# Pairs of tiles in the norms between blocks, and weight splits ahead of them, in a two-network fp32 kernel

## The reference

```python
for i in range(DEPTH):                      # DEPTH = 2
    mod = (c_act @ ada_w[i] + ada_b[i])[:, None, :]
    sh_m, sc_m, gt_m, sh_f, sc_f, gt_f = jnp.split(mod, 6, axis=-1)
    ...
    h = rmsnorm_2(x, norm_g[i, 0]) * (1.0 + sc_m) + sh_m
    y = rglru_mixer(h, ...) if i % 2 == 0 else gla_mixer(h, ...)
    x = x + gt_m * rmsnorm_2(y, norm_g[i, 1])
    h = rmsnorm_2(x, norm_g[i, 2]) * (1.0 + sc_f) + sh_f
    y = conv_ffn(h, ffn_w_up[i], ffn_conv_w[i], ffn_conv_b[i], ffn_w_down[i])
    x = x + gt_f * rmsnorm_2(y, norm_g[i, 3])
```

## Time and profile before

| | |
|---|---|
| median of 3 runs | 1875.89 us (1875.47 to 1876.12) |
| the profiled execution | 1869.09 us, its span 1867.3 us |
| PE busy | 1794.7 us (96%) |
| DVE busy | 1445.4 us (77%) |
| ACT busy | 885.7 us (47%) |
| granted TensorE clock, mean | 0.995 |

### The profile page before, as it was taken

How to read it: one execution, slowest core, us unless ns; L and a number is a source line. 1 busy time by engine, 2 the same in 40 slices (tenths; PEclk the granted TensorE clock), 3 DMA queues, 4 the chain that set the end, 5 groups by cost and what they waited for, 6 DMA issues and landing times.

```text
span 1867.3 us, 29958 instructions
## 1 busy us (share of the span) xinstructions
PE 1794.7 (96%) x11480; PEld 1583.2 (85%) x11480; DVE 1445.4 (77%) x2557; ACT 885.7 (47%) x1528; POOL 0.2 (0%) x4
## 2 busy tenths in 40 slices
PE   4999999999999999999999999998998999999997
PEld 2788887767888887988888999987998979989997
DVE  5649985558899988797867898777988888779864
ACT  3322334456222333443456555575665356556552
POOL 0000000000000000000000000000000000000000
PEclk8999999999999999999999999999999999999999
DMA  9422322113677776353222996443656924235652
GB/s 345 136 91 90 93 66 68 49 54 130 204 263 257 246 252 224 126 158 113 91 69 74 325 312 216 136 148 114 201 184 229 357 69 158 91 104 192 196 170 85
DMA packets 242909, 302.78 MB, mean 162 GB/s; under 512 B 6080, under 2 KB 224448, under 8 KB 242256
## 3 DMA queue, kind: packets, MB, share of 16 engines
q1 hardware_dynamic: 242768, 300.87, 48.8%
HBM read 299.79 MB, written 1.05 MB: 161 GB/s over the span
## 4 chain that ended last, share of the span: by engine, by line
PE 37%; DVE 12%; ACT 5%; issue 3%; DMA 1%; DVEq 0%; ACTq 0%
PE bank L567 8%; PE bank L562 8%; PE bank L564 8%; DVE w_lo L1744 3%; PE bank L538 3%; PE bank L540 3%; PE bank L539 3%; ACT w_hi L1129 2%; DVE work L2347 1%; DVE work L2353 1%; ACT work L1115 1%; DVE stats L1678 1%; PE bank L513 1%; DVE arena L2306 1%; PE bank L928 0%
## 5 line engine op out<-in xcount | busy, mean ns | idle before, releaser
L1744 DVE TENSOR_TENSOR w_lo<-ring,w_hi 128x1024 fp32r<-128x1024 f32 (+2 forms) x444 | 499.3, 1132 | 192.8 <-ACT w_hi L1129 189.5
L1129 ACT ACTIVATE w_hi<-ring 128x1024 fp32r<-128x1024 f32 (+2 forms) x444 | 433.9, 985 | 167.0 <-PE bank L567 102.7
L562 PE MATMUL bank<-h_hi,w_hi 128*128 128x256 f32 (+2 forms) x2374 | 419.2, 318 | 2.0 <-ACT w_hi L1129 1.6
L567 PE MATMUL bank<-h_hi,w_lo 128*128 128x256 f32 (+2 forms) x2374 | 411.4, 315 | 2.5 <-DVE w_lo L1744 2.5
L564 PE MATMUL bank<-h_lo,w_hi 128*128 128x256 f32 (+2 forms) x2374 | 411.4, 315 | 0.0
L562 PEld LDWEIGHTS bank<-h_hi,w_hi 128*128 128x128 f32 x2374 | 345.8, 188 | 36.1 <-ACT w_hi L1129 3.9
L567 PEld LDWEIGHTS bank<-h_hi,w_lo 128*128 128x128 f32 x2374 | 347.0, 188 | 32.4 <-DVE w_lo L1744 2.7
L564 PEld LDWEIGHTS bank<-h_lo,w_hi 128*128 128x128 f32 x2374 | 347.0, 188 | 29.9
L1115 ACT ACTIVATE work<-bank 128x512 f32<-128x512 f32 (+1 forms) x142 | 70.1, 507 | 280.8 <-PE bank L567 214.5
L1115 ACT ACTIVATE arena<-bank 128x256 f32<-128x256 f32 (+4 forms) x121 | 55.2, 457 | 221.1 <-PE bank L567 147.8
L538 PE MATMUL bank<-h_hi,w_hi 128*128 128x256 f32 (+2 forms) x426 | 127.0, 298 | 20.9 <-DVE h_lo L1697 9.1
(11 more groups left out here) (260 smaller groups left out, 2111.2 us busy)
## 6 DMA issues: line engine op xcount, KB each, us to landing
ring<-in_w_in SPq DMA_DIRECT2D x86, 1024.0 KB, 5.4
arena<-in_ada_w_t SPq DMA_DIRECT2D x96, 512.0 KB, 6.1
ring<-in_ffn_w_up SPq DMA_DIRECT2D x44, 1024.0 KB, 5.1
ring<-in_w_branch SPq DMA_DIRECT2D x32, 512.0 KB, 4.7
arena<-in_w_mod_t SPq DMA_DIRECT2D x32, 512.0 KB, 5.3
ring<-in_ffn_w_down SPq DMA_DIRECT2D x16, 1024.0 KB, 5.1
ring<-in_gla_w_in SPq DMA_DIRECT2D x12, 1024.0 KB, 5.4
ring<-in_w_out SPq DMA_DIRECT2D x8, 1024.0 KB, 5.4
```

Source lines behind the costliest of these rows:

```text
L562: pe.matmul(out[:, 0:n], w[0][:, k, :], hi(k, n), start=k == 0, stop=False)
L567: m = pe.matmul(out[:, 0:n], w[1][:, k, :], hi(k, n), start=False, stop=k == tiles - 1)
L1129: nc.scalar.activation(w_hi[u % PARTS][:, 0:src.shape[1], :], src, ACT.Copy)\
L1744: step(nc.vector.tensor_tensor(w_lo[u % PARTS][:, 0:nk, :], src, w_hi[u % PARTS][:, 0:nk, :].bitcast(F32), ALU.subtract), f"lo {u}", *(["u ...
```

## The change

1. `post` and `normed2` work on pairs of tiles. `post` becomes 8 tensor_tensor operations on 512 columns, with the reciprocal broadcast over the pair. The gain of y leaves `post`; ScalarE applies it in `store_y`, which now squares first and then stores with an Identity. In `normed2` the pairs are only multiplied by the reciprocal; ScalarE applies gain and shift in place, tile by tile, and makes `h_hi` of a pair with one copy. In the two ffn hand-overs (`single`) the first two tiles keep the old form.
2. ScalarE squares x in pairs; TensorE sums them in `sum_pairs`. Second fillers go from 11 (12 in hand-over 2) to 7 products.
3. The 16-wide z is made from the shifted tiles in full float32, 8 products in place of 16 on the parts.
4. VectorE makes the low parts of the next block's first three units (two in hand-over 2) ahead of `post`, the rest behind `normed2`. In hand-over 2 ScalarE makes the high parts of those two units ahead of the stores of the last two output tiles.

```diff
@@ -316,6 +316,12 @@
+        def two(t):
+            return t[:].rearrange("p (a s) -> p a s", a=2)
+        def pair_tile(k):
+            return dve_t[k // 2][:, S * (k % 2):S * (k % 2) + S]
@@ -613,6 +619,15 @@
+            def sum_pairs(name):
+                out = open_bank(name)
+                for k in range(KT):
+                    pe.wait_ge(*scalar.did(f"sq {name}.{k // 2}"))
+                    m = pe.matmul(out[:, 0:S], ones_pp, act_t[k // 2][:, S * (k % 2):S * (k % 2) + S],
+                                  start=k == 0, stop=k == KT - 1)
+                m.then_inc(*tensor.does("filled " + name))
@@ -866,8 +881,8 @@
                 keep_clock(9)
-                sum_all(f"n3 {l}", S, KT)
-                keep_clock(11)
+                sum_pairs(f"n3 {l}")
+                keep_clock(7)
@@ -942,14 +957,13 @@
             keep_clock(9)
-            sum_all("n2 1", S, KT)
-            keep_clock(12)
+            sum_pairs("n2 1")
+            keep_clock(7)
...
             for k in range(KT):
-                both_parts("n2 1")(k)
-                pe.matmul(out[0:16, 0:S], wz[:, k, :], h_hi[:, k, 0:S].bitcast(F32), start=k == 0, stop=False)
-                m = pe.matmul(out[0:16, 0:S], wz[:, k, :], h_lo[:, k, 0:S].bitcast(F32), start=False, stop=k == KT - 1)
+                pe.wait_ge(*scalar.did(f"shifted n2 1.{k}"))
+                m = pe.matmul(out[0:16, 0:S], wz[:, k, :], pair_tile(k), start=k == 0, stop=k == KT - 1)
@@ -959,7 +973,7 @@
                 for n in range(GLA_H):
-                    project(f"gla{nm} {n}", S)
+                    project(f"gla{nm} {n}", S, ready=both_parts("n2 1") if nm == "q" and n == 0 else None)
@@ -1489,25 +1503,42 @@
-            def pre_norm(name, ready, l, q, first):
+            def pre_norm(name, ready, l, q, first, single):
...
                 warm_sqrt(name)
-                square_all(name, S, KT, lambda k: xT[:, k, 0:S], ready)
+                for i in range(KT // 2):
+                    act.wait_ge(*ready(2 * i + 1))
+                    nc.scalar.activation(two(act_t[i]), xT[:, 2 * i:2 * i + 2, 0:S], ACT.Square)\
+                        .then_inc(*scalar.does(f"sq {name}.{i}"))
                 deviation(name, S, D)
-                modulated(name, (0,), lambda k, g: mod2[l][:, 12 * q + k:12 * q + k + 1])
-            def store_y(tag, k):
+                gain, shift = gain2[l][:, q, :], mod2[l][:, 12 * q:12 * q + KT]
+                for k in range(2 if single else 0):
+                    act.wait_ge(*vector.did(f"normed {name}.{k}"))
+                    nc.scalar.activation(h_hi[:, k, 0:S], pair_tile(k), ACT.Identity, bias=shift[:, k:k + 1])\
+                        .then_inc(*scalar.does(f"hi {name}.{k}"))
+                for k in range(2 if single else 0, KT, 2):
+                    act.wait_ge(*vector.did(f"normed {name}.{k}"))
+                    for i in (k, k + 1):
+                        a = nc.scalar.activation(pair_tile(i), pair_tile(i), ACT.Identity, scale=gain[:, i:i + 1],
+                                                 bias=shift[:, i:i + 1])
+                    a.then_inc(*scalar.does(f"shifted {name}.{k}", f"shifted {name}.{k + 1}"))
+                    act.wait_ge(*scalar.did(f"shifted {name}.{k}"))
+                    nc.scalar.activation(h_hi[:, k:k + 2, 0:S], two(dve_t[k // 2]), ACT.Copy)\
+                        .then_inc(*scalar.does(f"hi {name}.{k}", f"hi {name}.{k + 1}"))
+            def store_y(tag, k, l, q):
...
                 act.wait_ge(*tensor.did("filled " + name))
-                nc.scalar.activation(yT[:, k, :], bank(name)[:, 0:S], ACT.Copy)
-                nc.scalar.activation(sq8[:, k, :], bank(name)[:, 0:S], ACT.Square)\
-                    .then_inc(*scalar.does(name, "emptied " + name))
-            def block_out(tag, src, ready):
+                nc.scalar.activation(sq8[:, k, :], bank(name)[:, 0:S], ACT.Square).then_inc(*scalar.does(name))
+                nc.scalar.activation(yT[:, k, :], bank(name)[:, 0:S], ACT.Identity, scale=gain2[l][:, q, k:k + 1])\
+                    .then_inc(*scalar.does("emptied " + name))
+            def block_out(tag, src, ready, l):
...
                     first_units(f"y {tag}.0")
+                act.wait_ge(*vector.did(f"gain2 {l}"))
...
@@ -1556,8 +1587,10 @@
                         split_to(unit_of[f"down {l}.{c + 1}.0.1"])
+                    elif l == 0:
+                        split_to(unit_of["glaq 1"])
                     for j in range(2):
-                        store_y(f"ffn {l}", 2 * c + j)
+                        store_y(f"ffn {l}", 2 * c + j, l, 3)
...
@@ -1719,15 +1752,48 @@
-            def normed2(name, l, q):
+            def by_two(row):
+                return row.unsqueeze(1).broadcast_to([P, 2, S])
+            def normed2(name, l, q, single):
                 inverse(name, S)
-                tile, low = normed(name, (0,), lambda k, g: gain2[l][:, q, k:k + 1],
-                                   lambda k, g: mod2[l][:, 12 * q + k:12 * q + k + 1])
-                for k in range(KT + 2):
-                    if k < KT:
-                        tile(k)
-                    if k >= 2:
-                        low(k - 2)
+                def pair(k):
+                    step(nc.vector.tensor_tensor(two(dve_t[k // 2]), xT[:, k:k + 2, 0:S], by_two(stat2[:, 0:S]), ALU.mult),
+                         f"normed {name}.{k}")
+                def pair_low(k):
+                    dve.wait_ge(*scalar.did(f"hi {name}.{k}"))
+                    step(nc.vector.tensor_tensor(h_lo[:, k:k + 2, 0:S], two(dve_t[k // 2]),
+                                                 h_hi[:, k:k + 2, 0:S].bitcast(F32), ALU.subtract),
+                         f"lo {name}.{k}", f"lo {name}.{k + 1}")
+                def one(k):
+                    step(nc.vector.scalar_tensor_tensor(pair_tile(k), xT[:, k, 0:S], gain2[l][:, q, k:k + 1],
+                                                        stat2[:, 0:S], ALU.mult, ALU.mult), f"normed {name}.{k}")
+                def one_low(k):
+                    dve.wait_ge(*scalar.did(f"hi {name}.{k}"))
+                    step(nc.vector.scalar_tensor_tensor(h_lo[:, k, 0:S], pair_tile(k), mod2[l][:, 12 * q + k:12 * q + k + 1],
+                                                        h_hi[:, k, 0:S].bitcast(F32), ALU.add, ALU.subtract),
+                         f"lo {name}.{k}")
+                if single:
+                    one(0)
+                    one(1)
+                    pair(2)
+                    one_low(0)
+                    one_low(1)
+                    pair(4)
+                    pair_low(2)
+                    pair(6)
+                    pair_low(4)
+                    pair_low(6)
+                else:
+                    for k in range(0, KT, 2):
+                        pair(k)
+                    for k in range(0, KT, 2):
+                        pair_low(k)
@@ -2298,17 +2364,18 @@
-            def post(tag, l, q):
+            def post(tag):
                 inverse(f"ys {tag}", S)
-                for n in range(KT + 1):
+                for n in range(0, KT + 2, 2):
                     if n < KT:
-                        step(nc.vector.scalar_tensor_tensor(yT[:, n, :], yT[:, n, :], gain2[l][:, q, n:n + 1],
-                                                            stat2[:, 0:S], ALU.mult, ALU.mult), f"yn {tag}.{n}")
+                        step(nc.vector.tensor_tensor(yT[:, n:n + 2, :], yT[:, n:n + 2, :], by_two(stat2[:, 0:S]), ALU.mult),
+                             f"yn {tag}.{n}")
                     if n:
-                        k = n - 1
+                        k = n - 2
                         after(f"yn {tag}.{k}")
-                        step(nc.vector.tensor_tensor(xT[:, k, 0:S], xT[:, k, 0:S], yT[:, k, :], ALU.add), f"x {tag}.{k}")
+                        step(nc.vector.tensor_tensor(xT[:, k:k + 2, 0:S], xT[:, k:k + 2, 0:S], yT[:, k:k + 2, :], ALU.add),
+                             f"x {tag}.{k}", f"x {tag}.{k + 1}")
...
@@ -2325,11 +2392,11 @@
                     add_square(tag, k)
-                post(tag, l, 1)
+                split_to(unit_of[f"y {tag}.{KT - 1}"] + AHEAD)
+                post(tag)
             def ffn(l):
-                first_units(f"ffg {l}.0")
-                normed2(f"n3 {l}", l, 2)
+                normed2(f"n3 {l}", l, 2, True)
@@ -2377,9 +2444,10 @@
                 if l == 0:
+                    split_to(unit_of["glaq 1"])
...
                     settled()
-                post(f"ffn {l}", l, 3)
+                post(f"ffn {l}")
@@ -2457,14 +2525,15 @@
                 add_square("rg", k)
-            post("rg", 0, 1)
+            split_to(unit_of[f"y rg.{KT - 1}"] + AHEAD)
+            post("rg")
...
             settled()
+            step(nc.vector.memset(scan_one, 1.0), "scan_one")
+            normed2("n2 1", 1, 0, False)
             first_units("glaq 0")
-            step(nc.vector.memset(scan_one, 1.0), "scan_one")
```

(1 more changed line is left out.)

14 lines of the change are left out of this document (7 added, 7 removed).

## The result

| | before | changed |
|---|---|---|
| timed runs, median | 1875.68 us (1874.90 to 1876.12, 4 runs) | 1861.53 us (1859.23 to 1863.72, 4 runs) |
| profiled execution / span | 1869.09 / 1867.3 us | 1859.23 / 1857.4 us |
| granted clock of that execution | 0.995 | 0.993 |
| PE, DVE, ACT busy | 1794.7, 1445.4, 885.7 us | 1787.3, 1438.8, 892.9 us |

The profiled executions are only 9.9 us apart.

A forecast was written before the change was run, and what follows sets the result against it. The prediction took the chain of waits around the four hand-overs between blocks as the bound. Its terms, -2.97-4.57-2.97-0.85 = -11.36 us off a median of 1875.89, gave 1864.5 us, range 1860.5 to 1870.0.

The forecast's parts named there:

- three splits in VectorE's idle time: Sign, profile after: three weight splits stand in VectorE's idle time ahead of each block's first reciprocal.
- 0.10 us from root to reciprocal: Hand-overs 1 (recurrent block to ffn 0) and 3 (gated attention to ffn 1): this wait falls from 2.77 us, -2.67 each.
- z behind ScalarE: Hand-over 2 (ffn 0 to gated attention): gate's sum, fed by ScalarE's shifts, ends 8 us after its reciprocal, -0.98 us.
- the clock: Sign, profile after: TensorE's granted clock stays at 1.00 until the end.
- (a): Post and normed tiles: a pair costs as much as two single operations, +5.2 us together, 1869.7; chance 0.13.
- (b): Hand-over 2: the weight slab lands late and two stores wait behind its copies, 1866.2 us; chance 0.08.
- (c): Down projection of ffn 0: hand-over 1's 3 us are lost again to full DMA engines, 1867.5 us; chance 0.05.
- post and sum: Every hand-over: post in pairs and the sum of squares behind it, root's input read sooner, -0.35 us each.
- The square ahead of the copy: Every hand-over: squaring a stored tile before copying it shortens TensorE's wait for the last square, -0.17 us, four times.
- the end: Hand-over 4: post 1.01 and sum 0.17 us sooner, last transfer 0.33 later behind its data, -0.85 us.
- the difference is the same code, so I take the term off the median: Whole kernel: timed median lay 6.8 us above the profiled execution; -11.36 us was taken off 1875.89, giving 1864.5.
- Rival (d): First three hand-overs: with fewer fillers TensorE's clock falls once in each, +4.4 us, 1868.9; chance 0.07.

The follow-up runs named there:

- e10: The kernel before with 15 and 16 fillers in place of 11 and 12 behind the second sums: 1871.43 us against 1876.48, ratio 0.9980.
- e1: The kernel before with only the weight splits moved ahead of post: 1864.77 us against 1874.96, ratio 0.9948.
- e9: The changed kernel with VectorE's fifth split earlier, ScalarE's order in hand-over 2 changed and four output transfers: 1857.09 us, ratio to before 0.9899.
- e2: The changed kernel with the weight splits back behind post, its seven fillers kept: 1872.37 us against 1874.96 before, ratio 0.9983.
- e4: The changed kernel again, nothing altered: 1861.42 us, ratio to before 0.9931.
- e11: The changed kernel once more, nothing altered: 1862.54 us, ratio to before 0.9928.
- e8: The changed kernel with 4 and 5 fillers ahead of the ffns instead of 7, and hand-over 2's early weight splits put back late: 1863.71 us, ratio 0.9945.

## Why the prediction was right, and where its sizes were off

**The mechanism** was right at each point that the prediction named: three splits in VectorE's idle time, 0.10 us from root to reciprocal, post at 4.9 us, pair operations at 0.69, the first product 11.4 us after post began, z behind ScalarE. The sign that did not come out is the clock, which was to be 1.00 until the end: every trace of the changed kernel has stretches at 0.50 (1.2 GHz) from 1260 us on. Rivals (a), (b) and (c) did not come: 685 ns for a pair, copies in hand-over 2 done 1.0 us before the store was due, and what hand-over 1 gains is still there at hand-over 2 (196.89 and 197.23 us of work between in the two traces of before, 197.17 to 197.31 in the three of the changed kernel).

**The terms.** Forecast -2.97, -4.57, -2.97, -0.85; measured -2.83, -4.48, -2.84, -0.46. In hand-overs 1 and 3 post and sum gave 0.23 instead of 0.35: the last two pairs are released 0.6 us apart, no further than one square takes (0.63), so the last square queues. The square ahead of the copy gave 0.15 instead of 0.17. In hand-over 2 z gave 1.04 instead of 0.98. The largest miss is the end: I priced the second transfer of the last pair at the 0.33 us of spaced issues, and the tail grew by 0.73. Two issues back to back take some 0.9 us, and the last two pairs are released 0.60 apart, so the last pair also waits behind the one before it; that queue was not in the sum.

**The step that failed** is "the difference is the same code, so I take the term off the median". It did not carry the forecast out of its range, but the good fit of the time is partly luck: two errors, a gain 0.75 us too large in the hand-overs and one of nearly 4 us not forecast, run against each other. Off the profiled execution the sum gives 1857.7, against 1859.23; off the median 1864.5, against 1861.53. The 6.8 us between the two were no constant. e10 takes 3.7 us away by nothing but fillers in the pauses that the change shortens from 2.1 to 1.4 us. Rival (d) weighed clock falls as a new cost of the change; by e10's difference they were an old cost at the pauses of before, and a new one, by the traces, behind the gate's sum (3.3 and 3.0 us in two of three traces). A fall of some 3 us cost about what I took from the start of the trace or a little more (1.45 us there; 1.5 in e1, 1.6 in e9, 2.0 in e2), one of some 7 us 2.6 to 3.3 (e2, e4, e11). In sum -10.61 in the hand-overs and -3.7 from the pauses is -14.3 for the -14.15 timed. That it closes so well is luck: with the new falls behind the gate, 2.1 us in the mean of three traces, the sum is -12.2, and the interval of e10 alone is 3.5 us wide. Where the other 2 us come from stays open.

The rule of the Trainium skill that the prediction cites ("TensorE: Matmul & The Clock Gate", HAM oscillation), that waits between bursts of products bring the lower clock, is borne out in part: e2 and e8 have pauses of 3.26 and 2.70 us with a clock of 0.52 and 0.51 behind them, but 2.27 us in e8 and 2.51 in the first trace of before had none. It speaks against fewer fillers alone, as in e2; with the earlier splits the pauses became shorter, and it spoke for the change.
